# A hand-written order of steps for TensorE, VectorE and ScalarE, written anew

## The reference

```python
def reference(x, mem, ...):
    # first block, layer a:
    #   differential attention (6 heads, causal) + attention to 256 memory rows (4 heads)
    #   x = x + concat(o_self, o_mem) @ a_w_out
    #   x = x + relu(rms(x) @ a_w_up) ** 2 @ a_w_down          hidden width 4096
    # first block, layer b: keys and values from w_kv, rotary causal attention (12 heads),
    #   memory attention, output projection, the same kind of MLP, and a final RMS norm
    # second block:
    #   z = rms(x) @ w_in -> qa, c_kv, iq, ik, iw, qb, kb, vb, gb
    #   indexed sparse attention: index scores pick the 64 best keys of each query;
    #       8 heads with a relative bias attend to those
    #   retention of qb, kb, vb (8 heads), group norm, gain and bias, gated by silu(gb)
    #   x = x + concat(out_a, out_b) @ w_out
    #   x = x + (silu(h @ w_gate) * (h @ w_up)) @ w_down        hidden width 2816
```

## Time and profile before

| what | value |
|---|---|
| median of 3 runs | 915.58 us (914.89 to 916.04) |
| profiled execution, its span | 915.4 us |
| TensorE busy | 907.2 us |
| VectorE busy | 593.7 us |
| ScalarE busy | 490.4 us |
| GpSimd busy | 61.3 us |
| DMA moved | 159.88 MB, mean 175 GB/s |

### The profile page before, as it was taken

One profiled execution on the slowest core, in us unless ns is written; L12 is line 12 of the kernel. 1 busy time (PEld: TensorE's weight loads), 2 busy tenths in 40 slices (PEclk: granted clock), 3 DMA queues, 4 the chain that ended last, 5 costly groups with the idle time before them and its releaser, 6 DMA issues.

```text
span 915.4 us, 13523 instructions
## 1 busy us (share of the span) xinstructions
PE 907.2 (99%) x4824; PEld 767.8 (84%) x4824; DVE 593.7 (65%) x898; ACT 490.4 (54%) x750; POOL 61.3 (7%) x124
## 2 busy tenths in 40 slices
PE   9999999999999999999999999999999999999998
PEld 7778788888888888888888888888788888888887
DVE  4768858555555686746855555667987466555565
ACT  6756666444444566754644444465577464444452
POOL 1102122000000000000200000013130000000000
PEclk9999999999999999999999999999998999999999
DMA  8945137665555453424966555545441447556551
GB/s 297 335 139 183 49 138 236 212 196 183 183 188 193 168 176 103 134 97 149 328 204 197 199 186 184 148 137 197 170 161 43 142 139 230 184 183 188 190 172 47
DMA packets 96885, 159.88 MB, mean 175 GB/s; under 512 B 5969, under 2 KB 37921, under 8 KB 96841
## 3 DMA queue, kind: packets, MB, share of 16 engines
q1 hardware_dynamic: 94240, 155.08, 51.1%
q10 hardware_dynamic: 2568, 4.21, 1.3%
q0 software_dynamic: 32, 0.02, 0.0%
HBM read 158.21 MB, written 3.16 MB: 176 GB/s over the span
## 4 chain that ended last, share of the span: by engine, by line
PE 96%; DVE 2%; ACT 1%; issue 0%; POOL 0%; ACTq 0%; POOLq 0%; DVEq 0%
PE turn L1660 10%; PE proj L1660 9%; PE proj L1604 6%; PE proj L1606 6%; PE proj L1605 6%; PE score L1604 6%; PE score L1605 6%; PE score L1606 6%; PE outp L1604 5%; PE outp L1606 5%; PE outp L1605 5%; PE turn L1664 5%; PE proj L1664 5%; PE outp L1839 3%; PE score L1802 2%; PE turn L1650 2%
## 5 line engine op out<-in xcount | busy, mean ns | idle before, releaser
L1931 DVE TENSOR_TENSOR wlo<-raw,whi 128x2048 fp32r<-128x2048 f32 (+1 forms) x131 | 297.3, 2278 | 171.8 <-ACT whi L1350 132.7
L1350 ACT ACTIVATE whi<-raw 128x2048 fp32r<-128x2048 f32 x64 | 122.7, 1917 | 162.5 <-PE turn L1664 76.2
L1339 ACT ACTIVATE whi<-raw 128x2048 fp32r<-128x2048 f32 (+1 forms) x67 | 126.3, 1896 | 63.3 <-PE proj L1606 16.9
L1604 PE MATMUL proj<-whi,set 128*128 128x512 f32 (+1 forms) x270 | 106.6, 395 | 0.0
L1606 PE MATMUL proj<-whi,set 128*128 128x512 f32 (+1 forms) x270 | 103.8, 384 | 0.0
L1605 PE MATMUL proj<-wlo,set 128*128 128x512 f32 (+1 forms) x270 | 103.5, 383 | 0.0
L1660 PE MATMUL turn<-set,whi 128*128 128x512 f32 x384 | 96.3, 393 | 0.0
L1660 PE MATMUL proj<-set,whi 128*128 128x512 f32 x384 | 95.6, 391 | 0.0
L1604 PE MATMUL score<-whi,set 128*128 128x512 f32 x236 | 93.0, 394 | 0.0
L1605 PE MATMUL score<-wlo,set 128*128 128x512 f32 x236 | 92.1, 390 | 0.0
L1606 PE MATMUL score<-whi,set 128*128 128x512 f32 x236 | 92.0, 390 | 0.0
(11 more groups left out here) (231 smaller groups left out, 1318.5 us busy)
## 6 DMA issues: line engine op xcount, KB each, us to landing
raw<-in_a_w_up SPq DMA_DIRECT2D x32, 512.0 KB, 4.3
raw<-in_a_w_down SPq DMA_DIRECT2D x32, 512.0 KB, 4.5
raw<-in_b_w_up SPq DMA_DIRECT2D x32, 512.0 KB, 4.4
raw<-in_b_w_down SPq DMA_DIRECT2D x32, 512.0 KB, 4.5
raw<-in_w_gate SPq DMA_DIRECT2D x22, 512.0 KB, 4.0
raw<-in_w_up SPq DMA_DIRECT2D x22, 512.0 KB, 5.0
raw<-in_w_down SPq DMA_DIRECT2D x22, 512.0 KB, 4.1
raw<-in_a_w_in SPq DMA_DIRECT2D x20, 512.0 KB, 6.7
```

Source lines behind the costliest of these rows:

```text
L1339: return act.activation(shaped(whi, u)[:, ks, :], shaped(raw, u)[:, ks, :], ACT.Copy)
L1350: act.activation(shaped(whi, u), shaped(raw, u), ACT.Copy).then_inc(hi_done, 1)
L1604: pe.matmul(out_, hi, wh, start=start, stop=False)
L1931: return dve.tensor_tensor(shaped(wlo, u)[:, ks, :], shaped(raw, u)[:, ks, :], shaped(whi, u)[:, ks, :], ALU.subtract)
```

## The change

Only the three lists of `MOVES` differ: TensorE's grows from 53 pairs to 112, VectorE's from 70 to 155, ScalarE's from 65 to 137. Many of the new pairs give a place that the step had anyway. Of the 274 steps of TensorE 103 stand at another place, of VectorE's 281 steps 138, of ScalarE's 288 steps 196 (mostly by one or two places). GpSimd's and SP's programs are unchanged, as are all instructions inside a step. The diff, cut:

```diff
     "PE": [
...
-        ("retention_scores 3", "turn_heads 26"), ("multiply 67", "retention_scores 3"),
-        ("retention_scores 2", "retention_out 0"), ("multiply 66", "retention_scores 2"),
-        ("multiply 65", "multiply 66"), ("retention_scores 1", "multiply 64"), ("retention_scores 0", "multiply 63"),
...
+        ("split 52", "retention_out 1"), ("query_norm 0", "split 52"), ("evacuate 19", "query_norm 0"),
+        ("evacuate 18", "evacuate 19"), ("multiply 67", "evacuate 18"), ("retention_scores 2", "multiply 67"),
+        ("retention_out 0", "retention_scores 2"), ("multiply 66", "retention_scores 1"), ("split 51", "multiply 66"),
+        ("multiply 65", "split 51"), ("turn_heads 27", "retention_scores 0"), ("turn_heads 26", "turn_heads 27"),
+        ("index_scores 1", "multiply 59"), ("shared_key_sum 0", "multiply 58"), ("index_sum 0", "shared_key_sum 0"),
+        ("shared_kv 0", "index_sum 0"), ("index_scores 0", "shared_kv 0"), ("index_sum 1", "index_scores 0"),
+        ("turn_heads 23", "index_sum 1"), ("turn_heads 22", "turn_heads 23"), ("turn_heads 21", "multiply 57"),
+        ("turn_heads 20", "turn_heads 21"), ("split 35", "attend 30"), ("multiply 43", "split 35"),
...
+        ("multiply 4", "multiply 5"), ("turn_operand 5", "multiply 1"), ("turn_operand 4", "turn_operand 5"),
+        ("multiply 0", "turn_operand 4"),
     ],
     "DVE": [
...
-        ("split 53", "split 54"), ("exps 39", "mix 36"), ("exps 38", "exps 39"), ("turn_operand 33", "mix 33"),
-        ("turn_operand 32", "turn_operand 33"), ("exps 35", "turn_operand 32"), ("select 15", "exps 35"),
-        ("exps 34", "mix 32"), ("select 14", "exps 34"), ("group_gate 0", "select 14"), ("select 13", "group_gate 0"),
-        ("group_gain 0", "exps 32"), ("select 12", "group_gain 0"), ("group_scale 0", "select 12"),
...
-        ("rope_chunk 12", "split 47"), ("split 46", "small_norm 0"), ("statistics 5", "split 43"),
...
+        ("attend 32", "attend 33"), ("group_gate 0", "attend 32"), ("select 13", "exps 32"),
+        ("group_gain 0", "select 13"), ("group_scale 0", "group_gain 0"), ("select 12", "group_scale 0"),
...
+        ("statistics 5", "multiply 54"), ("split 42", "turn_operand 28"), ("multiply 50", "residual 12"),
...
-        ("evacuate 19", "query_norm 0"), ("evacuate 18", "evacuate 19"), ("retention_scores 2", "retention_out 0"),
-        ("split 52", "retention_scores 2"), ("retention_scores 1", "split 52"), ("split 51", "retention_scores 1"),
...
+        ("multiply 59", "split 45"), ("turn_heads 21", "multiply 59"), ("turn_heads 20", "turn_heads 21"),
+        ("split 43", "turn_operand 30"), ("multiply 54", "split 43"), ("statistics 5", "multiply 54"),
+        ("square_sum 5", "statistics 5"), ("up_first 3", "turn_operand 28"), ("late_loads 0", "up_first 3"),
+        ("split 42", "late_loads 0"), ("split 39", "turn_operand 26"), ("split 38", "turn_operand 24"),
```

## The result

The changed kernel takes 924.54 us in the median (924.12 to 925.67, 4 runs) against 915.81 (914.89 to 917.16, 4 runs): 1.0095 times as long, 95% interval 1.0084 to 1.0107, or 8.7 us slower. The prediction said slower, 918.7, within 913.0 to 922.0.

The account below looks back on a forecast made before the run. TensorE, 99% busy, was taken as the bound, so order matters only through its waits. Terms -0.3 - 0.2 + 1.7 + 1.0 + 1.1 - 0.2 = +3.1 gave span 918.5, time 918.7 us, range 913.0 to 922.0.

Parts of the forecast that it names:

- What bounds it: Whole kernel: TensorE, 99% busy, bounds it; order can give back at most 6.4 us, including 3.4 of clock.
- The start: Memory rows' second half turned before multiply 0, filling a 0.6 us TensorE wait: -0.3 us, between -0.6 and +0.5.
- Turns 14 and 15: Two operand turns ahead of attends 12 and 13, beside a 0.9 us wait: -0.2 us, between -0.9 and 0.
- Small heads: turn_heads 20, 21 now ahead of multiply 57: new TensorE wait for small_norm, +1.7 us, ends 0.5 and 2.5.
- Retention: Retention outs wait for GpSimd's masks beside three VectorE splits in a row: +1.0 us, including 0.3 for scores 2.
- a fall of the clock as a rival: Clock also falls behind the new wait at turn_heads 20: 3.4 us on top, 922, chance 0.13.
- Sparse attention: Select 13 ahead of the exps on VectorE lengthens the 1.5 us wait before scores 17: +1.1 us.
- The rest: The 60 to 112 us stretch, causal attention and transitions only swap ready neighbours: -0.2 us, from -0.7 to +0.5.
- From span to time: Whole kernel: 0.2 us added to the forecast span 918.5, as the runs' median exceeded the profile's span: 918.7.
- The rival with GpSimd in time: GpSimd's masks and statistics come in time, so no measurable change: 916.8 us, chance 0.27.
- the faster case: Denser sparse attention holds full clock from 688 us on, giving back 3.4 us: 913.1 us, chance 0.17.
- The rule that I weighed: VectorE and GpSimd share ports exclusively; waiting GpSimd would start at the next split boundary, retention term some 0.5; not relied on.

Follow-up runs that it names:

- late_old: Changed kernel with everything behind the second MLP, from statistics 5 on, in the order of before on three engines: 917.94 us.
- heads_old2: Changed kernel with the small heads' stretch on three engines, and TensorE's turn_heads 24 and 25, in the order of before: 923.03 us.
- exps5_first: Changed kernel with one step moved, exps 5 ahead of diff_norm 0 on VectorE: 923.71 us (one run).
- out2_late: Changed kernel with retention_out 2 behind multiply 68 on TensorE and retention_scores 3 ahead of it on ScalarE: 923.61 us.
- sel_back: Changed kernel with VectorE's group_scale ahead of select 12 and exps 32, 33 ahead of select 13, as before: 922.49 us.
- squares_first: Changed kernel with one step moved, split 16 behind attends 14 and 15 on ScalarE: 923.83 us (one run).
- norm5_between: Changed kernel with split 16 behind attend 15's squares on ScalarE and diff_norm 5 between splits 15 and 16 on VectorE: 923.3 us (one run).
- heads57: Changed kernel with turn_heads 20, 21 behind multiply 57 on TensorE and split 45 ahead of their evacuation on ScalarE: 927.47 us.

## Why the prediction had the direction right and the size wrong

- *What bounds it*: right. No work was added; 6.4 of the 7.5 us at equal clock are TensorE's waits, and 1.1 is tied to no run. The most that order can give back was put too high, since the 3.4 in it is clock and not time: 2.0 by late_old.
- *The start*, -0.3: -0.6 in the drift, at the edge of its bounds.
- *Turns 14 and 15*, -0.2 (to -0.9): the sign was wrong, +0.4. The 0.9 became 0.7, but turn_operand 8 now waits 0.31 for diff_norm 3, and two breaks were added.
- *Small heads*, +1.7: the wait is 1.45, and heads_old2 gets 1.9 back, of which 0.54 is half of the masks' wait. The chain of numbers held at each link that the rows show.
- *Retention*, +1.0: the waits are 1.28. But I let the clock out of this term. I had priced a fall of the clock as a rival and tied it to the small heads' wait, which never showed one, while it came behind the masks' shorter wait: 3.1 us of time in the profiled execution.
- *Sparse attention*, +1.1 between 1.0 and 1.8: +1.97 (3.48 - 1.51). "Select 12 keeps its place ahead of group_gain" was the slip: it kept the place in the list but not its company. Its 0.98 us had run beside GpSimd's L1313, for which it doesn't compete, and now L2298 did.
- *The rest*, -0.2 with at most +0.5: **the step that failed**. I wrote that these stretches "swap neighbours that are both ready, and no wait of before lies there". They cost 0.93 and 1.0 us of waits and 0.3 of breaks, 2.4 in the drift. The argument looked at whether the moved step's inputs were ready, not at what stood behind it on its engine: exps 5 came behind diff_norm 0's 1.30 us on VectorE (tested, exps5_first), and the squares of attend 15, with all that hangs on them, behind a later split 15 on ScalarE (read from rows). The prediction had named "a wait where I put none" as a sign that it is wrong; in these stretches there are three (0.29, 0.64 and 1.01). The causal attention was free, as said. So was late_loads: its issues stand at 602.2 and nothing waited for them.
- *The sum*: +3.1 against +8.7. By size: 2.6 in the rest, 0.6 in the turns at 113, 0.9 in the sparse attention, 0.3 in the retention's waits, and 1.2 between the medians by the clock, less 0.5 where the start and the small heads' wait did better; 0.5 is tied to no run.
- *From span to time*: the 0.2 that I added was no offset. It set a profiled execution at a clock of 0.996, span 915.4, against the median of three others, whose spans (their times less 1.7) were 913.2 to 914.3. An execution's time is its span and 1.7, so that 918.5 as a span at 0.996 is 920.2 as a time. It is much the same slip as the 1.2 by the clock: I took one execution's clock for the kernel's.
- *The rival with GpSimd in time* (916.8) fell with the masks; the faster case, full clock in the sparse attention, does occur, but in executions of before (16 of 68 had a mean clock of 1.000) and in none of the changed kernel's four; and it is worth 1.6 to 2.0 us, not 3.4. The clock's price made both ends of the range, 913.0 and 922.0.

The rule that I weighed, the exclusive lock of the Trainium skill's page "SBUF — State Buffer", section "SBUF: two separate sides", does better here than I let it: three of the four masks wait for the end of one split each and go, and the operation that came 0.02 us behind a split waited for all of it. Only L1249, now L1320 (618.98, with a boundary near 620.0, held to 622.25), passes a boundary between splits again, and no run here shows why.

## What to carry over

On an in-order queue a step that waits is as long as its wait for everything behind it: when steps are swapped, check not only whether the moved step's inputs are there but who stands behind it on each of the engines, and which operation of another engine it ran beside. Small GpSimd operations between two-input VectorE operations are such a wait: 0.2 us of work that may take 2.3. And a gap closed on the saturated engine gives nothing if the chain to the next join has its own length: out2_late moved 1.1 us from one wait into the next.

## What the runs showed that I had not expected

The low clock isn't bound to one place or one length. In the profiled execution of before it stood behind the late scores, 3.4 us of clock; 16 of 68 executions of the same kernel had a mean clock of 1.000 and ended only 1.6 us earlier. Behind the small heads' wait of 1.45 to 1.52 us it fell in none of nine profiles, and behind the masks' wait of 1.07 to 1.09 us in three of five (the changed kernel, sel_back, exps5_first; not in squares_first and norm5_between), and behind the 1.24 of heads57. What TensorE did ahead of the two waits differs: 128x292 and 128x512 multiplies there, and 128x64 and 64x256 ones among the 128x512 here. That this is the reason was not tested. A median of four executions therefore carries about 1 us of the clock's chance, and spans at equal clock separate kernels that medians can't.
